# The running sum of the squared residual at five layer boundaries: kept by GpSimd instead of VectorE

## The chip, the cores and the metric

The kernel runs on one core of one Trainium2 chip. The time is device microseconds of one launch, as the median of several runs. The engines are TensorE (PE; its weight loads are shown apart as PEld), VectorE (DVE), ScalarE (ACT), GpSimd (POOL) and SyncE (SP), which here only starts transfers. Each runs its own list of instructions in order; between engines there are semaphores, and an instruction waits until a semaphore has reached a number.

## The reference

Two layers of a decoder on 512 tokens with 1024 channels, all in fp32. Each layer is a half-step SwiGLU FFN, a token mixer (attention in layer 0, a convolution module in layer 1), and a second half-step FFN. Each of these six sublayers has a norm ahead and a norm behind, and adds to the residual h:

```python
def rms_norm(x, g):
    y = xf * lax.rsqrt(jnp.mean(xf * xf, axis=-1, keepdims=True) + NORM_EPS)
...
f = swiglu(rms_norm(h, norm_pre[i, 0]), w_ffn_in[i, 0], w_ffn_out[i, 0])
h = h + FFN_RES_WEIGHT * rms_norm(f, norm_post[i, 0])
t = rms_norm(h, norm_pre[i, 1])
...
h = h + rms_norm(t, norm_post[i, 1])
f = swiglu(rms_norm(h, norm_pre[i, 2]), w_ffn_in[i, 1], w_ffn_out[i, 1])
h = h + FFN_RES_WEIGHT * rms_norm(f, norm_post[i, 2])
```

So at each of the five boundaries between two sublayers the new residual is formed and its sum of squares over the 1024 channels is needed for every token.

## The kernel before

Activations lie transposed: 128 partitions hold 128 channels, the free dimension holds the 512 tokens, and the 1024 channels are eight chunks k = 0 to 7 (`KD = 8`). The residual is the tile `h_resid`, the output of a sublayer the tile `f_out`. fp32 products are made of three passes of matmuls: weights and activations are each split in a rounded part (`w_hi`, `x_hi`) and the rest (`w_lo`, `x_lo`). The weights come as a stream of slots of 128x1024 in a ring of four; ScalarE writes `w_hi` (L741), VectorE `w_lo` (L966), and TensorE multiplies eight blocks of 128 rows for each slot.

The work of all engines is in an order written by hand, with semaphores. A boundary (`boundary`, L1057 on VectorE, L803 on ScalarE) goes so. VectorE multiplies chunk k of `f_out` by the inverse norm in PSUM (`normalise`, L1065) and adds it to the residual (`add_residual`, L1070, which reads `f_out` and `h_resid`). ScalarE then writes `x_hi` of the chunk (L745) and the square of the residual (L747), which goes into the same chunk of `f_out`. VectorE writes `x_lo` (L983, which reads `h_resid` and `x_hi`). VectorE also adds the squares of chunks 1 to 6 into chunk 0, one addition per chunk (`add_h_square`, L992); chunk 7 is left to TensorE. VectorE's order in the loop is: normalise k, `x_lo` of k-1, residual k, add the square of k-1.

TensorE starts the next sublayer while that runs. `four_slots` (L366) takes chunk after chunk as it becomes ready and multiplies it with four weight slots: eight matmuls with `x_hi` (L379, L380), then four with `x_lo` (L383). After chunk 6 it sums the squares over the partitions (`columns`, L394, L357): it waits for the six additions (semaphore `h_sq_added`) and uses chunk 0 of `f_out`, then for the square of chunk 7. After the first two slots of chunk 7 it spreads the inverse norm (L363). The pre-norm factor is applied to the products later, so the matmuls don't wait for it.

Before the first sublayer there is no boundary; there VectorE adds the squares of the input in the main list (L1325). That part is the same in both kernels. GpSimd has only seven transfers of constants and some memsets, all at the start.

Of the kernel before, what the change touches and what calls it, by code (L numbers as in the profile page):

```python
# [34 lines left out]
ALU = mybir.AluOpType  # L35
# [6 lines left out]
KD = D // P  # L42
# [20 lines left out]
SUBS = 6  # L63
# [31 lines left out]
def build_program(nc, stream, xT, cols_in, rope_c, rope_s, perm_in, ident_in, ident_b_in, mask_in, taps_in, conv_in,  # L95
                  u_dram, z_dram, outT):
    ctx = ExitStack()
    with ctx:
        def sb(name, shape, dt=F32):
            return ctx.enter_context(nc.sbuf_tensor(name, shape, dt))  # L100

        def sem(name):
            return ctx.enter_context(nc.semaphore(name))
# [4 lines left out]
        f = sb("f_out", [P, KD, T])  # L108
# [77 lines left out]
        s_hsq, s_hacc = sem("h_squared"), sem("h_sq_added")  # L186
# [31 lines left out]
        def col(name, i):  # L218
            return cols[:, COLS[name] + i:COLS[name] + i + 1]
# [103 lines left out]
        @block.gpsimd  # L323
        def _(pool):
            pool.wait_ge(s_h0[KD - 1], 16)
            for dst, src in ((ident_b, ident_b_in), (ident, ident_in), (rc, rope_c), (rs, rope_s), (perm, perm_in)):
                pool.dma_start(dst[:, :], src[:, :]).then_inc(s_const, 16)
            pool.dma_start(mask[:, :, :], mask_in[:, :, :]).then_inc(s_const, 16)
            pool.dma_start(conv_c[:, :], conv_in[:, :]).then_inc(s_const, 16)
            for i in range(2):  # L330
                nc.gpsimd.memset(ug[:, i, :, 0:PAD], 0.0).then_inc(s_zeros, 1)

        CONSTS = 7 * 16

# [619 lines left out]
        def _(dve):  # L954
# [8 lines left out]
            def next_slot(n, s):  # L963

                dve.wait_ge(s_hi, n + RING + 1)
                nc.vector.tensor_tensor(w_lo[:, s, :], raw[:, s, :], w_hi[:, s, :].bitcast(F32), ALU.subtract  # L966
                                        ).then_inc(s_lo, 1)
# [7 lines left out]
            def invert(count):  # L975
                dve.wait_ge(s_root, count)
                if count > 1:
                    dve.wait_ge(s_bc, count - 1)
                on_diagonals(s_diag)

            def x_lo_of(sub, k):
                dve.wait_ge(s_xhi, KD * sub + k + 1)
                nc.vector.scalar_tensor_tensor(out=x_lo[:, k, :], in0=h[:, k, :], scalar=col("pre", sub * KD + k),  # L983
                                               in1=x_hi[:, k, :].bitcast(F32), op0=ALU.mult, op1=ALU.subtract
                                               ).then_inc(s_x, 1)

            def add_h_square(sub, k):

                dve.wait_ge(s_hsq, KD * sub + k + 1)
                if k > 1:  # L990
                    dve.wait_ge(s_hacc, (KD - 2) * sub + k - 1)
                nc.vector.tensor_tensor(f[:, 0, :], f[:, 0, :], f[:, k, :], ALU.add).then_inc(s_hacc, 1)  # L992
# [64 lines left out]
            def boundary(sub, n0):  # L1057

                invert(2 * sub + 2)
                if sub < SUBS - 1:  # L1060
                    next_slot(n0 - 1, RING - 1)
                dve.wait_ge(s_bc, 2 * sub + 2)

                def normalise(k):
                    nc.vector.tensor_tensor(f[:, k, :], f[:, k, :], BCAST[:, :], ALU.mult).then_inc(s_dve, 1)  # L1065
                    chain[0] += 1

                def add_residual(k):
                    dve.wait_ge(s_dve, chain[0])
                    nc.vector.scalar_tensor_tensor(out=h[:, k, :], in0=f[:, k, :], scalar=col("post", sub * KD + k),  # L1070
                                                   in1=h[:, k, :], op0=ALU.mult, op1=ALU.add).then_inc(s_h, 1)

                if sub == SUBS - 1:
                    for k in range(PE_OUT):
                        nc.vector.tensor_tensor(f[:, k, :], f[:, k, :], BCAST[:, :], ALU.mult).then_inc(s_fn, 1)
                    for k in range(PE_OUT, KD, 2):
                        normalise(k)
                        normalise(k + 1)
                        add_residual(k)
                        add_residual(k + 1)  # L1080
                    return
                for k in range(KD):
                    normalise(k)
                    if k:
                        x_lo_of(sub + 1, k - 1)
                    add_residual(k)
                    if k >= 2:
                        add_h_square(sub + 1, k - 1)
                x_lo_of(sub + 1, KD - 1)
                invert(2 * sub + 3)  # L1090
                next_slot(n0, 0)

            def ffn(n0, index, sub):
                n, q = n0, KF * index
                for g, chunks in enumerate(FFN_GROUPS):
                    if g == 0:
                        for p in range(2):
                            pair_steps(n + 2 * p, 2 * p, q + p, p, sub + 1, first=(p == 0))
                    with dve.Fori(1 if g == 0 else 0, 2 * chunks // RING) as i:
                        for p in range(2):  # L1100
                            pair_steps(RING * i + (n + 2 * p), 2 * p, 2 * i + (q + p), bass.ds(2 * i + p, 1),
                                       sub + 1)
                    n += 2 * chunks
                    down(n, "add" if g else "set", sub if g == len(FFN_GROUPS) - 1 else None)
                    n += KD
                    q += chunks
                boundary(sub, n0 + FFN_SLOTS)
# [223 lines left out]
            attention()  # L1331
            down(WO, "b_o", 1)
            boundary(1, FFN1)
            ffn(FFN1, 1, 2)
            ffn(FFN2, 2, 3)
            conv(PW1)
            down(PW2, "b_pw2", 4)
            boundary(4, FFN3)
            ffn(FFN3, 3, 5)

# [113 lines left out]
```

## Time and profile before

| | |
|---|---|
| median of 3 runs | 1917.95 us (1917.14 to 1918.6) |
| the profiled execution | 1919.01 us, its span 1916.3 us |
| TensorE busy | 1890.8 us, 99% of the span, at a granted clock of 0.999 |
| VectorE busy | 1019.1 us, 53% |
| ScalarE busy | 628.6 us, 33% |
| GpSimd busy | 4.2 us |
| additions of L992 | 36, of them 30 at the five boundaries |

Busy time is the time in which an engine had an instruction under way; TensorE's is modelled. The span runs from the first to the last instruction of the profiled execution; the time of the execution holds 2.7 us more, around it.

### The profile page before, as it was taken

Reading aid. Unit: us, or ns where it says so; the run is one execution under the profiler, and the core shown is the slowest. Engines: PE = TensorE matmul, PEld = TensorE weight load, DVE = VectorE, ACT = ScalarE, POOL = GpSimd, SP = SyncE. Lnnn points to the kernel's source line nnn. Section 1 sums busy time; section 2 is a strip of 40 time slices with the busy share of each in tenths; the row PEclk is TensorE's granted clock in tenths of the full one; section 3 lists DMA queues with packets and bytes.
Section 4 is the critical chain, followed back from the end, with each engine's and each line's share of the span. In section 5 each row is a group of like instructions: output and inputs, shape, how many; then the busy total and the mean of one; then the engine's idle time right before and its main releaser. Section 6 shows DMA issues by size and latency. Waiting matters only on the chain.

```text
span 1916.3 us, 24229 instructions
## 1 busy us (share of the span) xinstructions
PE 1890.8 (99%) x8989; PEld 1548.4 (81%) x8989; DVE 1019.1 (53%) x1393; ACT 628.6 (33%) x911; POOL 4.2 (0%) x13
## 2 busy tenths in 40 slices
PE   8999999999899999999999999999999999999998
PEld 6888888776578888888888888887898878888886
DVE  5434434687857434435754343457765674344345
ACT  5322213444534313223442222234112542232223
POOL 0000000000000000000000000000000000000000
PEclk9999999999999999999999999999999999999999
DMA  5332332321032332322233333232332223322321
GB/s 190 109 103 94 99 99 89 119 77 45 2 99 77 94 103 88 100 98 96 91 99 103 94 99 99 89 114 76 125 121 95 77 68 108 98 90 97 99 99 55
DMA packets 60849, 180.90 MB, mean 94 GB/s; under 512 B 6144, under 2 KB 15504, under 8 KB 60784
## 3 DMA queue, kind: packets, MB, share of 16 engines
q1 hardware_dynamic: 60432, 179.09, 29.1%
q8 instruction: 44, 0.72, 0.2%
q0 software_dynamic: 352, 0.92, 0.1%
q14 instruction: 21, 0.17, 0.0%
HBM read 173.69 MB, written 6.29 MB: 94 GB/s over the span
## 4 chain that ended last, share of the span: by engine, by line
PE 94%; DVE 4%; ACT 1%; issue 0%; DMA 0%; SPq 0%; DVEq 0%; ACTq 0%
PE bank L340 27%; PE bank L341 27%; PE bank L342 27%; PE bank L652 3%; PE bank L379 2%; PE bank L380 2%; PE bank L383 2%; PE bank L357 1%; DVE mx L1151 1%; PE bank L537 1%; DVE f_out L1167 1%; PE bank L660 1%; PE bank L515 0%; DVE w_lo L966 0%; DVE f_out L1176 0%
## 5 line engine op out<-in xcount | busy, mean ns | idle before, releaser
L966 DVE TENSOR_TENSOR w_lo<-w_raw,w_hi 128x1024 fp32r<-128x1024 f32 x312 | 381.5, 1225 | 456.1 <-ACT w_hi L741 445.3
L340 PE MATMUL bank<-x_hi,w_hi 128*128 128x512 f32 x1448 | 569.7, 393 | 0.8 <-DVE gate_tmp L999 0.2
L342 PE MATMUL bank<-x_hi,w_lo 128*128 128x512 f32 x1448 | 563.6, 389 | 0.0
L341 PE MATMUL bank<-x_lo,w_hi 128*128 128x512 f32 x1448 | 563.4, 389 | 0.0
L741 ACT ACTIVATE w_hi<-w_raw 128x1024 fp32r<-128x1024 f32 x312 | 328.8, 1056 | 611.9 <-PE bank L342 608.9
L340 PEld LDWEIGHTS bank<-x_hi,w_hi 128*128 128x128 f32 x1448 | 271.8, 188 | 61.5 <-issue 3.8
L340 PE MATMUL bank<-a_hi,w_hi 128*128 128x512 f32 (+1 forms) x844 | 320.7, 380 | 0.4 <-DVE w_lo L966 0.4
L341 PE MATMUL bank<-a_lo,w_hi 128*128 128x512 f32 (+1 forms) x844 | 320.0, 379 | 0.0
L342 PE MATMUL bank<-a_hi,w_lo 128*128 128x512 f32 (+1 forms) x844 | 319.9, 379 | 0.0
L341 PEld LDWEIGHTS bank<-x_lo,w_hi 128*128 128x128 f32 x1448 | 271.9, 188 | 58.1 <-issue 2.6
L342 PEld LDWEIGHTS bank<-x_hi,w_lo 128*128 128x128 f32 x1448 | 271.8, 188 | 56.7
L340 PEld LDWEIGHTS bank<-a_hi,w_hi 128*128 128x128 f32 x844 | 158.7, 188 | 32.3 <-DVE a_lo L1011 1.0
L341 PEld LDWEIGHTS bank<-a_lo,w_hi 128*128 128x128 f32 x844 | 158.7, 188 | 29.8
L342 PEld LDWEIGHTS bank<-a_hi,w_lo 128*128 128x128 f32 x844 | 158.7, 188 | 29.8
L999 DVE TENSOR_TENSOR up_tmp<-bank,r_pre 128x512 f32<-128x512 f32 x96 | 66.2, 690 | 191.4 <-PE bank L342 191.4
L772 ACT ACTIVATE a_hi<-up_tmp 128x512 f32 (+1 forms) x88 | 55.7, 633 | 276.9 <-DVE up_tmp L1009 276.9
L770 ACT ACTIVATE gate_tmp<-gate_tmp 128x512 f32<-128x512 f32 x88 | 55.7, 632 | 160.5 <-DVE gate_tmp L999 160.5
L1011 DVE TENSOR_TENSOR a_lo<-up_tmp,a_hi 128x512 f32 (+1 forms) x88 | 60.9, 692 | 80.0 <-ACT a_hi L772 80.0
L379 PE MATMUL bank<-x_hi,w_hi 128*128 128x512 f32 x168 | 67.3, 400 | 8.6 <-DVE w_lo L1322 7.6
L999 DVE TENSOR_TENSOR gate_tmp<-bank,r_pre 128x512 f32<-128x512 f32 x106 | 72.5, 684 | 0.0
L1009 DVE TENSOR_TENSOR up_tmp<-up_tmp,gate_tmp 128x512 f32<-128x512 f32 x88 | 60.9, 692 | 14.3 <-ACT gate_tmp L770 3.3
L380 PE MATMUL bank<-x_hi,w_lo 128*128 128x512 f32 x168 | 66.4, 395 | 0.0
(166 smaller groups left out, 1259.9 us busy)
## 6 DMA issues: line engine op xcount, KB each, us to landing
w_raw<-stream SPq DMA_DIRECT2D x312, 512.0 KB, 3.4
h_resid<-xT SPq DMA_DIRECT2D x8, 256.0 KB, 6.0
w_raw<-stream SPq DMA_DIRECT2D x8, 256.0 KB, 5.6
u_scratch<-V SPq DMA_DIRECT2D x8, 256.0 KB, 2.0
u_groups<-u_scratch SPq DMA_DIRECT2D x8, 256.0 KB, 2.8
qT<-z_scratch SPq DMA_DIRECT2D x8, 256.0 KB, 3.5
outT<-h_resid SPq DMA_DIRECT2D x8, 256.0 KB, 2.2
z_scratch<-kT SPq DMA_DIRECT2D x4, 256.0 KB, 2.3
```

The costliest lines, as they stand in the source:

```text
L340: nc.tensor.matmul(out, lw[0], lx[0], start=first, stop=False)
L341: nc.tensor.matmul(out, lw[0], lx[1], start=False, stop=False)
L342: return nc.tensor.matmul(out, lw[1], lx[0], start=False, stop=last)
L379: nc.tensor.matmul(bank[s][:, :], blk(w_hi, s, k), x[0][:, k, :], start=(k == 0), stop=False)
L380: nc.tensor.matmul(bank[s][:, :], blk(w_lo, s, k), x[0][:, k, :], start=False, stop=False)
L652: last = nc.tensor.matmul(bank[6 + j % 2][:, g * NT:(g + 1) * NT], mats[g][:, m, :, :].rearrange("p c q -> p (c q)"), ug[:, j % 2, g, m:m ...
L741: nc.scalar.activation(w_hi[:, s, :], raw[:, s, :], ACT.Copy).then_inc(s_hi, 1)
L770: nc.scalar.activation(g, g, ACT.Silu).then_inc(s_act, 1)
L966: nc.vector.tensor_tensor(w_lo[:, s, :], raw[:, s, :], w_hi[:, s, :].bitcast(F32), ALU.subtract).then_inc(s_lo, 1)
L999: nc.vector.tensor_tensor(dst, bank[s][:, :], r_pre[:, :], ALU.mult).then_inc(s_evac, 1)
L1009: nc.vector.tensor_tensor(U[:, p, :], U[:, p, :], G[:, p, :], ALU.mult).then_inc(s_prod, 1)
L1011: nc.vector.tensor_tensor(a_lo[:, chunk, :], U[:, p, :], a_hi[:, chunk, :].bitcast(F32), ALU.subtract).then_inc(s_a, 1)
```

## The change

The call of `add_h_square` leaves VectorE's loop over the chunks of a boundary. GpSimd gets the same 30 additions, five times six, behind its memsets, each with the same two waits: for the square of the chunk, and from the second on for the addition before. The semaphore that TensorE waits for is raised by GpSimd now, to the same numbers.

```diff
@@ gpsimd @@
+            def add_h_squares(sub):
+                for k in range(1, KD - 1):
+                    pool.wait_ge(s_hsq, KD * sub + k + 1)
+                    if k > 1:
+                        pool.wait_ge(s_hacc, (KD - 2) * sub + k - 1)
+                    nc.gpsimd.tensor_tensor(f[:, 0, :], f[:, 0, :], f[:, k, :], ALU.add).then_inc(s_hacc, 1)
+
+            for sub in range(1, SUBS):
+                add_h_squares(sub)
@@ vector, boundary @@
                     if k:
                         x_lo_of(sub + 1, k - 1)
                     add_residual(k)
-                    if k >= 2:
-                        add_h_square(sub + 1, k - 1)
                 x_lo_of(sub + 1, KD - 1)
```

On VectorE, in the loop of a boundary, from the residual of chunk 1 to the residual of chunk 3, the order before was this:

```order
L1070 SCALAR_TENSOR_TENSOR h_resid<-f_out,cols,h_resid 128x512
L1065 TENSOR_TENSOR f_out<-f_out,bank 128x512
L983 SCALAR_TENSOR_TENSOR x_lo<-h_resid,cols,x_hi 128x512
L1070 SCALAR_TENSOR_TENSOR h_resid<-f_out,cols,h_resid 128x512
L992 TENSOR_TENSOR f_out<-f_out 128x512
L1065 TENSOR_TENSOR f_out<-f_out,bank 128x512
L983 SCALAR_TENSOR_TENSOR x_lo<-h_resid,cols,x_hi 128x512
L1070 SCALAR_TENSOR_TENSOR h_resid<-f_out,cols,h_resid 128x512
```

The same place in the changed kernel, whose lines have numbers higher by 10 (`bank` is the PSUM bank with the inverse norm):

```order
L1080 SCALAR_TENSOR_TENSOR h_resid<-f_out,cols,h_resid 128x512
L1075 TENSOR_TENSOR f_out<-f_out,bank 128x512
L993 SCALAR_TENSOR_TENSOR x_lo<-h_resid,cols,x_hi 128x512
L1080 SCALAR_TENSOR_TENSOR h_resid<-f_out,cols,h_resid 128x512
L1075 TENSOR_TENSOR f_out<-f_out,bank 128x512
L993 SCALAR_TENSOR_TENSOR x_lo<-h_resid,cols,x_hi 128x512
L1080 SCALAR_TENSOR_TENSOR h_resid<-f_out,cols,h_resid 128x512
```

The addition between the residual of a chunk and the next normalise is gone; nothing else of VectorE's list moved. On GpSimd, the end of the list in the changed kernel:

```order
L328 DMA mask<-mask_in 128x512
L329 DMA conv_consts<-conv_in 128x192
L331 MEMSET u_groups 128x4x8 x2
L338 ISA
L338 TENSOR_TENSOR f_out<-f_out 128x512 x30
L98 UNCONDITIONAL_BRANCH
```

Before, the list ended with the memsets; the 30 additions stand behind them, and nothing stands behind the additions.

## Rows read from the trace of the kernel before

**Rows 1.** The page: busy time of each engine, and TensorE's granted clock.
```profile
PE 1890.8 (99%) x8989; PEld 1548.4 (81%) x8989; DVE 1019.1 (53%) x1393; ACT 628.6 (33%) x911; POOL 4.2 (0%) x13
...
PEclk9999999999999999999999999999999999999999
```

**Rows 2.** TensorE's waits: us in total, times, longest.
```profile
PE bank L379 <- DVE w_lo L1322: 7.6, 1, 7.6
...
PE bank L379 <- ACT x_hi L745: 1.0, 5, 0.3
```

**Rows 3.** Windows over the five boundaries: us, busy time of each engine.
```profile
376.00:403.00 27.00, 26.84 (x122) 20.45 (x122) 21.96 (x35) 11.46 (x19) 0.00 (x0) 1.00 0.07 20
569.00:597.00 28.00, 27.68 (x126) 20.89 (x125) 22.78 (x35) 12.38 (x20) 0.00 (x0) 1.00 0.05 20
...
1534.00:1561.00 27.00, 26.84 (x123) 20.59 (x123) 21.99 (x34) 11.38 (x19) 0.00 (x0) 1.00 0.06 20
```

**Rows 4.** Timeline of VectorE, attention's boundary: start, duration, idle before.
```profile
378.07 0.75 DVE L1070 SCALAR_TENSOR_TENSOR h_resid<-f_out,cols,h_resid 128x512 f32<-128x512 f32 x1
378.75 0.68 DVE L1065 TENSOR_TENSOR f_out<-f_out,bank 128x512 f32<-128x512 f32 x1
379.62 0.75 DVE L983 SCALAR_TENSOR_TENSOR x_lo<-h_resid,cols,x_hi 128x512 fp32r<-128x512 f32 x1 [0.20 <-ACT x_hi L745]
380.29 0.74 DVE L1070 SCALAR_TENSOR_TENSOR h_resid<-f_out,cols,h_resid 128x512 f32<-128x512 f32 x1
...
382.50 0.74 DVE L1070 SCALAR_TENSOR_TENSOR h_resid<-f_out,cols,h_resid 128x512 f32<-128x512 f32 x1
383.16 0.68 DVE L992 TENSOR_TENSOR f_out<-f_out 128x512 f32<-128x512 f32 x1
...
385.02 0.75 DVE L1070 SCALAR_TENSOR_TENSOR h_resid<-f_out,cols,h_resid 128x512 f32<-128x512 f32 x1
...
395.78 0.70 DVE L992 TENSOR_TENSOR f_out<-f_out 128x512 f32<-128x512 f32 x1
...
400.99 0.18 DVE L971 RECIPROCAL r_col<-root_col 128x4 f32<-128x4 f32 x1 [3.58 <-ACT root_col L753]
```

**Rows 5.** Timeline of ScalarE, same boundary.
```profile
379.49 0.62 ACT L747 ACTIVATE f_out<-h_resid 128x512 f32<-128x512 f32 x1
381.07 0.73 ACT L745 ACTIVATE x_hi<-h_resid,cols 128x512 fp32r<-128x512 f32 x1 [0.96 <-DVE h_resid L1070]
381.70 0.62 ACT L747 ACTIVATE f_out<-h_resid 128x512 f32<-128x512 f32 x1
...
393.38 0.73 ACT L745 ACTIVATE x_hi<-h_resid,cols 128x512 fp32r<-128x512 f32 x1 [1.28 <-DVE h_resid L1070]
394.01 0.62 ACT L747 ACTIVATE f_out<-h_resid 128x512 f32<-128x512 f32 x1
```

**Rows 6.** Timeline of TensorE and its weight loads, same boundary.
```profile
382.27 0.19 PEld L379 LDWEIGHTS bank<-x_hi,w_hi 128*128 128x128 f32 x1
...
395.19 1.07 PE L383 MATMUL bank<-x_lo,w_hi 128*128 128x512 f32 x4
397.91 1.07 PE L383 MATMUL bank<-x_lo,w_hi 128*128 128x512 f32 x4
398.59 1.98 PEld L357 LDWEIGHTS bank<-ones,f_out 128*128 128x128 f32 x16
```

**Rows 7.** Line L992: ns min/median/max, first and last start.
```profile
L992 DVE TENSOR_TENSOR f_out<-f_out x36: 680/689/696, 10.5 to 1553.6; 128x512 f32<-128x512 f32 x36
```

**Rows 8.** GpSimd's groups: busy us, mean ns.
```profile
L331 POOL MEMSET u_groups<- 128x32 f32 x2 | 0.2, 144 | 0.0
L1447 POOL MEMSET const-float32-0.0<- 128x1 f32 x1 | 0.1, 99 | 0.3 <-issue 0.3
```

## The prediction

> **What bounds the kernel now.** I read the shares first. TensorE is busy for 99% of the span and its clock is granted in full in every slice; VectorE is at 53%, GpSimd at nothing [rows 1]. So time taken from VectorE is worth something only where TensorE waits for VectorE. The list of TensorE's waits comes next: its longest entry lies before the first boundary, in the start of the program, and its waits for `x_hi`, the only input that a boundary feeds it chunk by chunk, sum to 1.0 us in five waits [rows 2]. There are five boundaries, so these are the waits for chunk 0, one in each, and chunk 0 is ready before any of the moved additions runs. The windows say the same from the other side: in a boundary of 27 us TensorE is busy for 26.84, and the five look alike, so that one can stand for all [rows 3].
>
> Then the race within a boundary. TensorE takes one chunk in 2.72 us (395.19 to 397.91) [rows 6]. VectorE takes 2.21 us for a chunk without the addition (residual at 378.07, 380.29, 382.50) and 2.52 us with it (382.50 to 385.02) [rows 4]. The addition itself lasts 0.69 us [rows 7], but the cycle grows by 0.31 only, since without it VectorE idles 0.20 us for `x_hi` and overlaps less. Either way it is faster than TensorE. In numbers: `x_hi` of chunk 1 is ready at 381.07 + 0.73 = 381.80 [rows 5], and TensorE asks for it at 382.27 [rows 6], 0.47 us later. `x_hi` of chunk 6 is ready at 394.11 [rows 5], and TensorE asks for it at 382.27 + 5 x 2.72 = 395.87, 1.76 us later. The margin grows with each chunk.
>
> **The change part by part.** Removed: 30 additions of 0.69 us, 20.7 us of VectorE. At a boundary the cycle falls from 2.52 to at best 2.21 us, and `x_hi` of chunk 6 comes at 381.80 + 5 x 2.21 = 392.85 in place of 394.11. TensorE is not waiting there, so this is worth 0. Behind the loop nothing is gained either: VectorE stands idle for 3.58 us until the root [rows 4], and that root comes after TensorE's column sums. The stall that would be next is TensorE's own rate.
>
> Added: 30 additions on GpSimd. The trace shows no such operation on that engine, so I bound it. Below: no faster than VectorE's 0.69 us [rows 7]. Above: the memset of 32 elements took 144 ns and that of one took 99 [rows 8], 1.45 ns an element for a single stream of writes; an addition has two streams in and one out, and three times 1.45 ns for 512 elements plus 0.1 us is 2.3 us. The one-stream price gives 0.84 us. I take 1.3 us, an estimate half-way between this and the sum of two such streams (1.6), rounded up for the handling of semaphores. The whole of it lies beside other work if the chain of six ends before TensorE's column sums, whose first weight load starts at 398.6 [rows 6]. The first square is ready at 381.70 + 0.62 = 382.32 [rows 5], so each addition may take (398.6 - 382.3) / 6 = 2.7 us before TensorE waits, above even my upper bound of 2.3. At 1.3 us the chain isn't the limit at all: the last addition follows the square of chunk 6, which ends 0.52 us after its `x_hi` [rows 5], near 393.4, and is done near 394.8. Before, it was done at 395.78 + 0.70 = 396.5 [rows 4]. Nothing is queued behind the additions on GpSimd; its transfers and memsets are ahead of them, in the first 20 us of the program, long over. Cost: 0.
>
> What is left is whether an addition on GpSimd slows VectorE, for both then work from the same memory at the same time. No row of before can show it: GpSimd does nothing in all five windows [rows 3]. From below: no effect, and no gain from one, so 0. From above I work it out as a full block. In VectorE's cycle the instruction for `x_lo` starts 1.55 us after the residual's start and ends 2.30 after it; the next residual starts 2.22 after it; the square is ready at 379.49 + 0.62 = 380.11, which is 2.04 after [rows 4, 5]. GpSimd's addition is thus ready just ahead of the next residual. If that residual waits for the whole addition, the cycle is 2.04 + 0.05 + 1.3 = 3.4 us. With a cycle p, `x_hi` of chunk 6 is ready at 381.80 + 5p and wanted at 395.87, so TensorE loses 5p - 14.07 us in each boundary: nothing up to p = 2.81, and 2.9 us at 3.4. Five boundaries give 14.7 us. With an addition of 0.69 us p is 2.78 and the loss 0; with 2.3 us p is 4.4 and the loss 7.9 x 5 = 40 us. If instead VectorE's residual goes first and the addition fits behind it, it starts about 0.75 us after the residual's start, ends at 2.05, and moves `x_lo` from 1.55 to there: p = 2.05 + 0.67 = 2.7, below 2.81, loss 0. I take this second order or a weaker slowdown, 0, since it needs no more than that VectorE's instructions, which come back to back, aren't parted.
>
> On this the Trainium skill speaks against the change. SBUF — State Buffer, "Who interferes with whom", says that VectorE instructions with two SBUF inputs share a read interface with GpSimd instructions that read SBUF, that it is held for a whole instruction, and that the one that comes second waits. L1070 and L983 have two such inputs; L1065 has one in PSUM. By that page the block above is the mechanism, and its order of arrival is what decides between p = 3.4 and p = 2.7. It also gives a price: GPSIMD Engine Reference, "Elementwise — side-by-side cycle accounting", has 4497 ns for an addition of 2048 fp32 elements, by which 512 would be an estimated 1.1 us; the block would then be p = 3.2 and 9.7 us in all. No run here shows either yet.
>
> The sum against the profiled execution: span 1916.3 + 0, with 2.7 around it 1919.0 as before. The median of the runs lies 1.1 below that execution, so I forecast 1918.0 us.
>
> **The rivals.**
>
> 1. GpSimd gets in ahead of the residual each time and blocks it (p near 3.4). For it: the square is ready 0.18 us before the residual starts. Against it: with handling on GpSimd the start may come after it; and where the two orders alternate (one residual unhindered at 2.21, the next waiting behind both, near 3.9), the average is 3.1, with chunk 5 ready at 381.80 + 2 x 2.21 + 2 x 3.9 = 394.0 against 393.15 wanted, a loss near 0.9 us, 4 us in all. Full block: 1918.0 + 14.7 = 1932.7 us. It decides from p = 2.81.
>
> 2. GpSimd's addition is itself near its upper bound of 2.3 us, and VectorE goes first but `x_lo` waits: it starts at 0.75 + 2.3 = 3.05 after the residual, p = 3.7, a loss of 4.4 us per boundary, 1940 us. For it: only the scaling of a memset. Against it: that the small memset has a fixed part.
>
> 3. The relief of VectorE is worth something: faster. The most that could come back is the 1.0 us of `x_hi` waits [rows 2], and these lie ahead of the additions. 1917 us at best; no row supports more.
>
> 4. Sharing stretches VectorE's instructions instead of blocking them: some 0.3 to 0.6 us in a cycle, p = 2.5 to 2.8, no loss. It belongs to the forecast.
>
> **How the numbers follow.** A measurement of this kernel tells about 0.2%, 3.8 us, from no change. No change that counts: 0.58 (this holds the forecast, rival 4, and a part of the alternating case). Rival 1 with its alternating form above 3.8 us: 0.30. Rival 2: 0.08. Faster by more than 3.8 us: 0.04, for what I haven't seen. So faster 0.04, same 0.58, slower 0.38. The likeliest case alone is 1915.5 to 1921; the range must reach over rival 1 at 1932.7, with a little more, and leaves out rival 2: 1915.5 to 1934.
>
> **What would show each step.** VectorE should have 30 instructions fewer and its busy time should be near 1019.1 - 20.7 = 998.4 us, if nothing is stretched; more than that is rival 4. GpSimd should have 30 additions, with starts at least 1.1 to 1.5 us apart where they follow at once. The starts of the residual's instruction give p: 2.2 to 2.7 confirms the forecast, 3.1 or more is rival 1, and then the idle time of TensorE before L379 (L389 in the new numbering) for `x_hi` grows from 1.0 us to 4 to 15. The column sums must not wait for the sixth addition. In case of a block the instruction that comes late shows which order the two engines took: the residual late by about an addition is rival 1, `x_lo` late by some 0.5 us the forecast. The prediction is wrong if TensorE waits at a chunk other than chunk 0 in any boundary.

## The result, and the profile after

The changed kernel takes 1928.31 us (1927.26 to 1930.03, 4 runs) against 1917.55 us (1916.99 to 1918.6, 4 runs): the ratio is 1.0057, with a 95% interval of 1.0043 to 1.0071. It is 10.8 us slower. That lies in the stated range, but it isn't the case that I had held the likeliest; it is the first rival.

The page of the changed kernel, busy time of each engine (its lines are numbered higher by 10 from L340 on, and by 8 behind VectorE's boundary):

```profile
PE 1895.2 (98%) x8977; PEld 1547.8 (80%) x8989; DVE 1034.5 (54%) x1363; ACT 627.6 (33%) x911; POOL 44.4 (2%) x43
```

VectorE has 30 instructions fewer than in [rows 1] and is busy for 15.4 us more. Two groups say where, the first of VectorE, the second of GpSimd (one line each of the changed kernel: ns min/median/max, first and last start):

```profile
L1080 DVE SCALAR_TENSOR_TENSOR h_resid<-f_out,cols,h_resid x44: 743/1782/1793, 379.0 to 1921.9; 128x512 f32<-128x512 f32 x44
```
```profile
L338 POOL TENSOR_TENSOR f_out<-f_out x30: 1331/1338/1345, 383.3 to 1564.5; 128x512 f32<-128x512 f32 x30
```

The residual's instruction, 0.75 us in [rows 4], lasts 1.78 us at the median. The same stretch of attention's boundary as in [rows 4], in the changed kernel, VectorE first, then GpSimd (start, duration):

```profile
381.19 0.75 DVE L1080 SCALAR_TENSOR_TENSOR h_resid<-f_out,cols,h_resid 128x512 f32<-128x512 f32 x1
...
382.73 0.75 DVE L993 SCALAR_TENSOR_TENSOR x_lo<-h_resid,cols,x_hi 128x512 fp32r<-128x512 f32 x1 [0.19 <-ACT x_hi L755]
383.40 1.78 DVE L1080 SCALAR_TENSOR_TENSOR h_resid<-f_out,cols,h_resid 128x512 f32<-128x512 f32 x1
385.11 0.67 DVE L1075 TENSOR_TENSOR f_out<-f_out,bank 128x512 f32<-128x512 f32 x1
385.98 0.75 DVE L993 SCALAR_TENSOR_TENSOR x_lo<-h_resid,cols,x_hi 128x512 fp32r<-128x512 f32 x1 [0.20 <-ACT x_hi L755]
386.64 1.78 DVE L1080 SCALAR_TENSOR_TENSOR h_resid<-f_out,cols,h_resid 128x512 f32<-128x512 f32 x1
```
```profile
383.30 1.33 POOL L338 TENSOR_TENSOR f_out<-f_out 128x512 f32<-128x512 f32 x1 [362.75 <-ACT f_out L757]
386.54 1.33 POOL L338 TENSOR_TENSOR f_out<-f_out 128x512 f32<-128x512 f32 x1 [1.91 <-ACT f_out L757]
```

Read the starts together: GpSimd's addition starts at 383.30, VectorE's residual at 383.40, 0.10 us behind, and it lasts 1.03 us longer than alone. The cycle of a chunk is 386.64 - 383.40 = 3.24 us, where it was 2.52. `x_lo` and the normalise keep their lengths. It is the same for each of the six additions of each of the five boundaries: GpSimd is ahead by 0.10 or 0.11 us, and the residual lasts 1.78 or 1.79.

What that does to TensorE, in the changed kernel: its waits (us, times, longest), and three weight loads: of the first matmul of attention's boundary, of the first of a later chunk, and of the first column sum. Behind them stands the first matmul's weight load in the kernel before:

```profile
PE bank L389 <- DVE w_lo L1330: 8.4, 1, 8.4
PE bank L389 <- ACT x_hi L755: 5.0, 24, 0.3
```
```profile
380.54 0.19 PEld L389 LDWEIGHTS bank<-x_hi,w_hi 128*128 128x128 f32 x1 [0.66 <-ACT x_hi L755]
...
392.47 0.19 PEld L389 LDWEIGHTS bank<-x_hi,w_hi 128*128 128x128 f32 x1 [0.64 <-ACT x_hi L755]
...
401.60 2.10 PEld L367 LDWEIGHTS bank<-ones,f_out 128*128 128x128 f32 x16
```
```profile
379.64 0.19 PEld L379 LDWEIGHTS bank<-x_hi,w_hi 128*128 128x128 f32 x1 [0.66 <-ACT x_hi L745]
```

The waits for `x_hi` are no longer five but 24, four or so more in each boundary, for the later chunks [rows 2]. Their sum of 5.0 us is too small, because matmuls under way cover part of an idle stretch: at the later chunk above the weight load waited for 0.64 us. (The wait for `w_lo` lies in the start of the program, before any of the moved additions.) The distance from the first weight load to the column sums shows the loss whole: 401.60 - 380.54 = 21.06 us, and before 398.59 [rows 6] - 379.64 = 18.95. So about 2.1 us are lost in this boundary, and 2.09 to 2.11 in each of the other four. The five sum to 10.5 us. Up to the spreading of the inverse norm, with the wait for chunk 7 in it, it is 2.21 to 2.23 us a boundary, 11.1 in all. Measured were 10.8: the loss lies here.

### The profile page after: what moved, and what is told of

Read it like the earlier page. It is cut to its first block, busy times and chain, and to the rows that moved or that the text cites. A ratio compares the mean times of both kernels' runs of the same rounds, so it can differ in the third digit from the quotient of the medians.

```text
span 1926.6 us, 24219 instructions
## 1 busy us (share of the span) xinstructions
PE 1895.2 (98%) x8977; PEld 1547.8 (80%) x8989; DVE 1034.5 (54%) x1363; ACT 627.6 (33%) x911; POOL 44.4 (2%) x43
## 4 chain that ended last, share of the span: by engine, by line
PE 89%; DVE 8%; ACT 2%; issue 1%; DMA 0%; SPq 0%; DVEq 0%; ACTq 0%
PE bank L350 27%; PE bank L352 26%; PE bank L351 26%; PE bank L662 3%; DVE h_resid L1080 3%; ACT x_hi L755 1%; DVE x_lo L993 1%; PE bank L367 1%; PE bank L389 1%; PE bank L390 1%; PE bank L393 1%; DVE mx L1159 1%; PE bank L547 1%; DVE f_out L1175 1%; PE bank L670 1%
## 5 line engine op out<-in xcount | busy, mean ns | idle before, releaser
L352 PE MATMUL bank<-x_hi,w_lo 128*128 128x512 f32 x1448 | 564.3, 390 | 0.0
L338 POOL TENSOR_TENSOR f_out<-f_out 128x512 f32<-128x512 f32 x30 | 40.1, 1338 | 1505.2 <-ACT f_out L757 1505.2
```

The lines of the kernel that those rows point to most:

```text
L352: return nc.tensor.matmul(out, lw[1], lx[0], start=False, stop=last)
```

## The experiments

Theory A: GpSimd's addition, once it has started, holds up a VectorE instruction that has two inputs in SBUF, and TensorE pays only for a cycle above 2.81 us. The rivals are named in each expectation. All comparisons are with the kernel before on the same chip.

**Neither engine adds.**

```diff
-            for sub in range(1, SUBS):
-                add_h_squares(sub)
@@ tensor, columns @@
-                    pe.wait_ge(s_hacc, (KD - 2) * sub + KD - 2)
+                    if sub == 0:
+                        pe.wait_ge(s_hacc, KD - 2)
+                    else:
+                        pe.wait_ge(s_hsq, KD * sub + KD - 1)
```

> Left out: the additions of chunks 1 to 6 at the five boundaries, on either engine, so that only chunks 0 and 7 enter the norm there. Theory A (GpSimd's addition, once started, holds up a VectorE instruction that has two inputs in SBUF): taking the additions from VectorE is worth nothing by itself; the residual's instruction lasts 0.75 us, the cycle of a chunk is 2.21 us, the time that of before, 1917.5 us (+- 2). Rival D (the additions on VectorE also cost TensorE something that the waits don't show): 2 to 5 us faster than before.

Measured: 1916.46 us against 1917.1, ratio 0.9999 (0.999 to 1.0009). Residuals of this kernel's VectorE, two after one another:

```profile
382.88 0.74 DVE L1081 SCALAR_TENSOR_TENSOR h_resid<-f_out,cols,h_resid 128x512 f32<-128x512 f32 x1
...
385.09 0.75 DVE L1081 SCALAR_TENSOR_TENSOR h_resid<-f_out,cols,h_resid 128x512 f32<-128x512 f32 x1
```

The cycle is 2.21 us, and the 20.7 us taken from VectorE are worth nothing. Rival D falls.

**GpSimd waits for the next residual.**

```diff
                     pool.wait_ge(s_hsq, KD * sub + k + 1)
+                    pool.wait_ge(s_h, KD * (sub - 1) + k + 2)
```

> The changed kernel, with GpSimd's addition of chunk k also waiting until the residual of chunk k+1 is written. Theory A: the residual's instruction is back at 0.75 us; the addition starts some 0.1 us behind it, beside the normalise (one input in PSUM, not held up), and holds up the next x_lo, which would start 0.8 us later, until 1.13 us after its own start: x_lo's instruction lasts about 1.2 us in place of 0.75. Cycle near 2.65 us, below the 2.81 from which TensorE waits: 1917.5 us. Rival B (the two engines share the memory and slow each other whenever they overlap, whoever came first): the normalise is stretched too, GpSimd's addition lasts longer than 1.34 us, cycle 2.7 to 3.0, 1917.5 to 1922 us. Rival C (the additional instructions in GpSimd's chain or the later semaphore make TensorE wait): no change against the changed kernel, 1928.

Measured: 1916.45 us against 1917.1, ratio 0.9995 (0.9985 to 1.0004). VectorE and GpSimd in this kernel:

```profile
385.38 0.74 DVE L1081 SCALAR_TENSOR_TENSOR h_resid<-f_out,cols,h_resid 128x512 f32<-128x512 f32 x1
386.05 0.67 DVE L1076 TENSOR_TENSOR f_out<-f_out,bank 128x512 f32<-128x512 f32 x1
386.91 1.18 DVE L994 SCALAR_TENSOR_TENSOR x_lo<-h_resid,cols,x_hi 128x512 fp32r<-128x512 f32 x1 [0.20 <-ACT x_hi L756]
388.02 0.74 DVE L1081 SCALAR_TENSOR_TENSOR h_resid<-f_out,cols,h_resid 128x512 f32<-128x512 f32 x1
```
```profile
386.25 1.29 POOL L339 TENSOR_TENSOR f_out<-f_out 128x512 f32<-128x512 f32 x1 [1.34 <-DVE h_resid L1081]
```

The addition, from 386.25 to 387.54, lies over most of the normalise (0.67 us, as ever) and the start of `x_lo`, which is what lasts longer now: 1.18 us. Cycle 2.64, time of before. The whole loss is gone with all 30 additions still on GpSimd, as theory A has it; rivals B and C fall.

**GpSimd starts just behind the residual instead of just ahead.**

```diff
                     pool.wait_ge(s_hsq, KD * sub + k + 1)
+                    pool.wait_ge(s_x, KD * sub + k + 1)
```

> The changed kernel, with GpSimd's addition of chunk k also waiting until x_lo of chunk k is written, 0.26 us later than the square. The next residual has then started some 0.1 us before. Theory A: who starts first holds the other up. The residual lasts 0.75 us, the addition's reads start only when the residual is done, 0.6 us after its semaphore; it then holds up the next x_lo by 0.3 to 0.5 us. Cycle 2.5 to 2.7, 1917.5 us. Rival B (shared whoever came first): the residual, overlapped by the addition for 0.65 of its 0.75 us, still lasts 1.3 to 1.7 us; cycle 2.9 to 3.2, 1921 to 1927 us. A third way, in which GpSimd wins whoever came first: the residual is interrupted, 1.7 us or more, 1928 us.

Measured: 1916.77 us against 1917.1, ratio 1.0003 (0.9993 to 1.0013).

```profile
384.78 0.74 DVE L1081 SCALAR_TENSOR_TENSOR h_resid<-f_out,cols,h_resid 128x512 f32<-128x512 f32 x1
...
386.31 0.92 DVE L994 SCALAR_TENSOR_TENSOR x_lo<-h_resid,cols,x_hi 128x512 fp32r<-128x512 f32 x1 [0.20 <-ACT x_hi L756]
387.15 0.74 DVE L1081 SCALAR_TENSOR_TENSOR h_resid<-f_out,cols,h_resid 128x512 f32<-128x512 f32 x1
```
```profile
384.99 1.69 POOL L339 TENSOR_TENSOR f_out<-f_out 128x512 f32<-128x512 f32 x1 [0.68 <-DVE x_lo L994]
```

This is the pair to put beside the changed kernel. There the addition starts 0.10 us ahead of the residual, and the residual lasts 1.78 us. Here it starts 0.21 us behind; the residual lasts 0.74, and the addition takes 1.69 us in place of 1.34. Whoever starts second waits. The cycle is 2.37 us, a little under what I had expected.

**The residual reads PSUM.**

```diff
-                    nc.vector.tensor_tensor(f[:, k, :], f[:, k, :], BCAST[:, :], ALU.mult)...
+                    out = f[:, k, :] if last else bank[6 + k % 2][:, :]
+                    if not last and k >= 2:
+                        dve.wait_ge(s_h, KD * sub + k - 1)
+                    nc.vector.tensor_tensor(out, f[:, k, :], BCAST[:, :], ALU.mult)...
@@ add_residual @@
-                    ... in0=f[:, k, :], ...
+                    ... in0=f[:, k, :] if last else bank[6 + k % 2][:, :], ...
```

`last` is true only in the last sublayer, behind which there is no boundary; it keeps the SBUF tile. TensorE's filler matmuls behind the spreading write to bank 0 in place of 7.

> The changed kernel, with the normalised chunk written to a PSUM bank (two banks in turn) instead of back to its SBUF tile at the five boundaries, so that the residual's instruction has one input in SBUF and one in PSUM. GpSimd's addition still starts just ahead of it. Theory A: a VectorE instruction with one input in SBUF isn't held up. The residual lasts 0.75 us beside an addition of 1.34 us, x_lo starts after the addition and lasts 0.75, cycle 2.2 to 2.3 us, 1917.5 us. Rival B (shared memory, any overlap): the residual stays above 1.2 us, 1923 to 1928 us. Rival E (both use the tile f_out, and that is what collides): the same 0.75 us as theory A, since the residual no longer reads that tile; the run with other tiles tells E apart.

Measured: 1916.64 us against 1917.1, ratio 1.0003 (0.9994 to 1.0013).

```profile
386.82 0.75 DVE L1085 SCALAR_TENSOR_TENSOR h_resid<-bank,cols,h_resid 128x512 f32<-128x512 f32 x1
```
```profile
386.72 1.34 POOL L338 TENSOR_TENSOR f_out<-f_out 128x512 f32<-128x512 f32 x1 [0.86 <-ACT f_out L757]
```

GpSimd is 0.10 us ahead, as in the changed kernel, and both keep their full speed. One input in SBUF isn't held up. Rival B falls for good.

**Other tiles.**

```diff
-                    nc.gpsimd.tensor_tensor(f[:, 0, :], f[:, 0, :], f[:, k, :], ALU.add)
+                    nc.gpsimd.tensor_tensor(spare[:, 0, :], spare[:, 0, :], spare[:, 1, :], ALU.add)
```

(`spare` is in the tile `tap_matrix`, which is used only in the convolution.)

> Left out: the sum of the squares of chunks 1 to 6. The changed kernel, with each of GpSimd's additions made of the same size and at the same points, but on a spare tile that nothing else uses. Theory A (an addition with inputs in SBUF holds up a VectorE instruction with two inputs in SBUF, whatever the tiles): the residual still lasts 1.78 us, cycle 3.24, 1928 us, as the changed kernel. Rival E (both engines reading the tile f_out is what collides): residual 0.75 us, cycle 2.2, 1917.5 us.

Measured: 1928.43 us against 1916.75, ratio 1.0052 (1.0035 to 1.0068).

```profile
384.94 1.78 DVE L1084 SCALAR_TENSOR_TENSOR h_resid<-f_out,cols,h_resid 128x512 f32<-128x512 f32 x1
...
388.18 1.78 DVE L1084 SCALAR_TENSOR_TENSOR h_resid<-f_out,cols,h_resid 128x512 f32<-128x512 f32 x1
```
```profile
384.84 1.33 POOL L342 TENSOR_TENSOR tap_matrix<-tap_matrix 128x512 f32<-128x512 f32 x1 [1.90 <-ACT f_out L761]
```

The residuals last 1.78 us, the cycle is 3.24: the changed kernel's loss, with no tile in common. Rival E falls.

**Write only.**

```diff
+                    nc.gpsimd.memset(spare[:, 0, :], 0.0)
```

> Left out: the sum of the squares of chunks 1 to 6. As the run with the spare tile, but GpSimd writes the 128x512 with a memset instead of adding. Theory A in its narrow form (the interface that both engines read through is what is held): a memset reads nothing, the residual lasts 0.75 us, cycle 2.2, 1917.5 us. Rival F (any access of GpSimd to SBUF holds VectorE up): the residual lasts 0.75 plus most of the memset, 1.2 us or more.

Measured: 1916.53 us against 1916.75, ratio 0.9998 (0.9988 to 1.0007).

```profile
386.21 0.75 DVE L1084 SCALAR_TENSOR_TENSOR h_resid<-f_out,cols,h_resid 128x512 f32<-128x512 f32 x1
```
```profile
386.08 0.53 POOL L342 MEMSET tap_matrix<- 128x512 f32 x1 [1.62 <-ACT f_out L761]
```

The memset lies over the first 0.40 us of the residual and costs it nothing. Held up as it is beside GpSimd's reading instructions (their time plus 0.44 us, see the table below), it would have lasted about 0.97 us. So it is reading that collides. Rival F falls.

**One input.**

```diff
+                    nc.gpsimd.tensor_copy(spare[:, 0, :], spare[:, 1, :])
```

> Left out: the sum of the squares of chunks 1 to 6. As the run with the spare tile, but GpSimd copies 128x512 instead of adding: one input in place of two. Theory A: it still reads, so it still holds the residual up, for its own time. If the reads set the time of the hold (1.13 us for two inputs), near half: residual 1.2 to 1.4 us, cycle 2.65 to 2.8, below the 2.81 from which TensorE waits, 1917.5 to 1919 us. If one input costs as much as two: 1.78 and 1928 us. Rival G (only two-input operations of GpSimd collide): residual 0.75.

Measured: 1917.47 us against 1916.75, ratio 1.0 (0.999 to 1.0009). The copy takes 0.68 us and the residual beside it 1.10. It collides, for its own shorter time; rival G falls. Cycle 2.56 us, and no loss.

**Twice the size.**

```diff
+                    nc.gpsimd.tensor_tensor(extra[:, 0:2 * T], extra[:, 0:2 * T], extra[:, 0:2 * T], ALU.add)
```

> Left out: the sum of the squares of chunks 1 to 6. As the run with the spare tile, but each addition has 1024 elements a partition. Theory A and the formula for the loss, (5p - 14.07) x 5: the addition lasts 2.5 us, the residual waits about 2.2 us and lasts 2.9, cycle p = 2.21 + 2.1 = 4.3 to 4.4, 37 to 40 us slower than before, 1955 to 1958 us. Rival B' (a hold of fixed length per instruction, not by its size): residual 1.78, 1928 us.

Measured: 1947.8 us against 1916.75, ratio 1.0161 (1.0143 to 1.0179), 31 us.

```profile
387.31 2.38 DVE L1084 SCALAR_TENSOR_TENSOR h_resid<-f_out,cols,h_resid 128x512 f32<-128x512 f32 x1
...
391.15 2.38 DVE L1084 SCALAR_TENSOR_TENSOR h_resid<-f_out,cols,h_resid 128x512 f32<-128x512 f32 x1
```
```profile
387.21 1.94 POOL L342 TENSOR_TENSOR tap_matrix<-tap_matrix 128x1024 f32<-128x1024 f32 x1 [1.91 <-ACT f_out L761]
```

A miss in size. The addition takes 1.94 us, not 2.5; both of its inputs are the same block here, and whether that is why was not tested by itself (the next run speaks for it). The cycle is 3.84, the formula gives (5 x 3.84 - 14.07) x 5 = 25.7 us, and up to the column sums, which is as far as the formula reaches, the five boundaries lose 25.6. A new wait comes on top: TensorE's column sums now wait for the square of chunk 7 (2.8 us in five waits). In attention's boundary, from the first `x_hi` matmul to the spreading, 28.15 us pass, and 22.31 before: 5.84 more. Three other boundaries lose 5.81, and the second 6.88, for a reason that stays open: 30.1 us in all, beside the 31 measured. The hold of a fixed length, rival B', falls.

**Two additions in a row.** A second one on the spare tile stands behind each:

```diff
                     nc.gpsimd.tensor_tensor(f[:, 0, :], f[:, 0, :], f[:, k, :], ALU.add).then_inc(s_hacc, 1)
+                    ...
+                    nc.gpsimd.tensor_tensor(spare[:, 0, :], spare[:, 1, :], spare[:, 1, :], ALU.add)
```

> The changed kernel, with a second addition of 128x512 on a spare tile behind each of GpSimd's additions, waiting for nothing. The residual has by then been waiting since GpSimd's first addition. Theory A1 (whoever asked first is next): the residual goes between the two, lasts 1.78 us; the second addition runs beside the normalise and holds up the next x_lo by about 0.3 us. Cycle near 3.55 us, loss (5 x 3.55 - 14.07) x 5 = 18 us, 1936 us. Theory A2 (GpSimd keeps its turn as long as it has instructions): the residual waits for both, 2.9 us or more, cycle 4.4, loss 40 us, 1957 us.

Measured: 1928.75 us against 1916.71, ratio 1.006 (1.0043 to 1.0077).

```profile
385.96 1.79 DVE L1088 SCALAR_TENSOR_TENSOR h_resid<-f_out,cols,h_resid 128x512 f32<-128x512 f32 x1
387.67 0.68 DVE L1083 TENSOR_TENSOR f_out<-f_out,bank 128x512 f32<-128x512 f32 x1
388.54 0.75 DVE L1001 SCALAR_TENSOR_TENSOR x_lo<-h_resid,cols,x_hi 128x512 fp32r<-128x512 f32 x1 [0.19 <-ACT x_hi L763]
```
```profile
385.85 1.34 POOL L342 TENSOR_TENSOR f_out<-f_out 128x512 f32<-128x512 f32 x1 [0.46 <-ACT f_out L765]
387.16 1.49 POOL L346 TENSOR_TENSOR tap_matrix<-tap_matrix 128x512 f32<-128x512 f32 x1
```

The second addition doesn't get ahead of the waiting residual (1.79 us, as with one): the order is A1's, and A2 falls. But this is no test of who is next when both wait. The residual ends at 387.75, thus reads from about 387.00 on, and the second addition starts only at 387.16: it comes second here. It is the one that lasts longer, 1.49 us. It ends 0.90 us after the residual, where the addition of two different blocks in the run behind `x_lo` ended 1.16 after it (386.68 against 385.52). This addition has the same block twice, as the 1024 one had, and both were shorter than two different blocks would lead one to expect. What I had added for `x_lo`, 0.3 us, isn't there: the second addition reads mostly beside the normalise and is over 0.1 us after `x_lo` starts. Sixty additions cost what thirty cost.

**Half the size, and three quarters.**

```diff
+                    nc.gpsimd.tensor_tensor(f[:, 0, 0:T // 2], f[:, 0, 0:T // 2], f[:, k, 0:T // 2], ALU.add)
```

> Left out: the squares of chunks 1 to 6 for the last 256 tokens. The changed kernel, with additions of 128x256. Theory A with a hold in proportion to the size: the addition lasts 0.7 to 0.75 us, the residual 0.75 + 0.4 to 0.5 = 1.15 to 1.25 us, cycle 2.6 to 2.7 us, below 2.81, so the whole loss is gone although the hold isn't: 1917.5 us. A rival in which a loss follows the hold in proportion: half the loss, 1923 us.

Measured: 1916.95 us against 1916.71, ratio 0.9999 (0.9989 to 1.0008). Addition 0.78 us, residual 1.23, cycle 2.69: almost half the hold, none of the loss. Then with `3 * T // 4`:

> Left out: the squares of chunks 1 to 6 for the last 128 tokens. The changed kernel, with additions of 128x384, between the size that cost nothing (256: residual 1.23 us, cycle 2.69) and the full one (512: residual 1.78 us, cycle 3.24, 10.8 us). The hold in proportion to the size: residual 1.50 us, cycle 2.97. Theory A with a threshold, (5p - 14.07) x 5: 3.9 us slower than before, 1921 us. A loss in proportion to the hold, without a threshold, can no longer be (256 cost nothing); a loss that steps in whole additions would be 0 or 10.8.

Measured: 1920.39 us against 1917.03, ratio 1.0013 (1.0004 to 1.0022), thus 2.5 us (0.8 to 4.2); the medians differ by 3.4.

```profile
386.49 1.50 DVE L1081 SCALAR_TENSOR_TENSOR h_resid<-f_out,cols,h_resid 128x512 f32<-128x512 f32 x1
...
389.45 1.50 DVE L1081 SCALAR_TENSOR_TENSOR h_resid<-f_out,cols,h_resid 128x512 f32<-128x512 f32 x1
```

The cycle is 2.96 us, and the formula's (5 x 2.96 - 14.07) x 5 = 3.7 us lies in the interval. From the first `x_hi` matmul to the column sums TensorE takes 19.67 us, 0.72 more than before, 3.6 us in five. Together the runs in which GpSimd comes first (us; the measured loss is taken by the ratio, which makes 10.9 of the changed kernel's 10.8):

| GpSimd's instruction | its time | residual | cycle p | formula | measured |
|---|---|---|---|---|---|
| memset 512 | 0.53 | 0.75 | 2.21 | 0 | -0.4 |
| copy 512 | 0.68 | 1.10 | 2.56 | 0 | 0 |
| add 256 | 0.78 | 1.23 | 2.69 | 0 | -0.2 |
| add 384 | 1.06 | 1.50 | 2.96 | 3.7 | 2.5 |
| add 512 | 1.34 | 1.78 | 3.24 | 10.7 | 10.9 |
| add 1024, one block twice | 1.94 | 2.38 | 3.84 | 25.7 | 31 |

The residual's time is that of GpSimd's reading instruction plus 0.44 us, within 0.02, in every line but the first. (The 512 addition on other tiles lost 10.0 us and the two in a row 11.5, at the same cycle of 3.24.) Told by the ends: a held-up instruction of 0.75 us ends 0.54 or 0.55 us after GpSimd's. That holds for the held-up `x_lo` too, 388.09 against 387.54 in the run in which GpSimd waits for the next residual, and 387.23 against 386.68 in the run behind `x_lo`. No version beats the kernel before: those that avoid the loss (behind the residual, behind `x_lo`, through PSUM) are equal to it, since the relief of VectorE is worth nothing here.

## Why the prediction was right, and where it wasn't

The range and the structure held; the choice of the likeliest case did not. The forecast of 1918.0 us is 10.3 too low, and the range held only because it reached over rival 1, to which I had given 0.30.

- *What bounds the kernel.* Right. TensorE's pace of 2.72 us a chunk hides VectorE's cycle up to 2.81, and leaving the additions out gave nothing.
- *GpSimd's own time.* 1.3 us estimated, 1.34 measured. As predicted the chain of additions was not the limit: the sixth starts at 399.51, is over at 400.85, and the column sums start at 401.60.
- *"I take this second order or a weaker slowdown, 0."* This step failed. The trace of before had put the square 0.18 us ahead of the residual, which spoke for GpSimd; I set that aside with a delay for handling that no row showed, and with the thought that VectorE's back-to-back instructions wouldn't be parted. That delay is 0.08 us (the square ends at 382.60 + 0.62 = 383.22, the addition starts at 383.30), less than the 0.18, and GpSimd started 0.10 us ahead, 30 times of 30. The run in which it starts some 0.21 us behind the residual costs nothing, so it was this order that decided between 1917 and 1928 us.
- *Rival 1.* Its mechanism was right and one term was too large: the cycle measured 3.24 us, not 3.4. I had let the residual wait for the whole addition; it waits until 0.2 us before the end (it ends at 385.18, thus reads from about 384.43 on, and the addition ends at 384.63; the profile calls spans on GpSimd rough, so that the 0.2 us is less sure than the cycle). With 3.24 the formula gives 10.7 us, with 3.4 it had given 14.7. Its alternating form was not seen: with GpSimd's addition over before the next `x_lo`, each cycle starts from the same position.
- *Rival 2* fell with the measured 1.34 us, and rival 3 with the run without additions. *Rival 4* (stretched, not blocked) fell with the run behind `x_lo`, where the residual keeps 0.74 us beside an addition under way.
- *VectorE's busy time.* Predicted 998.4 us if nothing was stretched, measured 1034.5: 30 x 1.03 = 31 us of it are residuals that stand waiting. The other 5 us are for the most part an error of the sum: the additions had overlapped their neighbours, so that their removal takes less than 20.7 us. The run without additions has 1002.6 us, 16.5 less than before.

The rule of the Trainium skill that I had weighed and set against my own choice (SBUF — State Buffer, "Who interferes with whom") is what the runs showed: a VectorE instruction with two inputs in SBUF is held up (1.78 us), one with an input in PSUM is not (0.75), a GpSimd instruction that only writes holds nothing up (0.75), and the one that starts second waits (1.69 us for the addition when it was second). The same page of the Trainium skill, in its section "SBUF: two separate sides", lets the one that starts first keep the interface for its whole instruction. That is a little more than these traces show, where the last 0.2 us of GpSimd's addition are free. The estimate of 1.1 us from the Trainium skill's GPSIMD Engine Reference, "Elementwise — side-by-side cycle accounting", was under the measured 1.34.

## What to carry to other kernels

Moving an elementwise instruction to an idle GpSimd isn't free for VectorE: look for VectorE instructions with two SBUF inputs that start within GpSimd's instruction, and put their end behind GpSimd's (those of 0.75 us ended 0.55 us behind it here). Then hold the new cycle against the pace of the bounding engine: here everything up to 2.81 us was free, and everything above it was paid for five times in each of five boundaries. If it is over, one more wait that lets the other engine start first, or an operand in PSUM, takes the collision away without moving the work back.

When two engines become ready within 0.2 us of each other, take the order that the trace shows and not the one that seems kinder; I had that row and argued past it.

## What was new about the hardware

- GpSimd's addition takes 0.78, 1.06 and 1.34 us for 256, 384 and 512 elements a partition: 2.2 ns an element and 0.22 us fixed. Its copy of 512 takes 0.68, its memset 0.53.
- A held-up instruction shows its wait as its own duration, on either engine (the residual's 1.78, the addition's 1.69 us), and not as idle time. No view of waits names it; only an instruction that lasts longer than its like does.
- In one of the five boundaries (the last) of the run in which GpSimd waits for the next residual, the first `x_lo` that is held up lasted 1.54 us in place of 1.19. Why stays open.
